# Last down projection: 14 of 22 k tiles of three pairs of output tiles as a block product by seven products

## The reference

```python
def conv_glu_ffn(xn, w_up, conv_w, conv_b, w_down):
    u = causal_dwconv3(xn @ w_up, conv_w) + conv_b
    gate, up = jnp.split(u, 2, axis=-1)
    return (jax.nn.silu(gate) * up) @ w_down
...
        x = x + conv_glu_ffn(rmsnorm(x, ffn_norm[layer]), ffn_w_up[layer], ffn_conv_w[layer],
                             ffn_conv_b[layer], ffn_w_down[layer])
```

## Time and profile before

| | us |
|---|---|
| median of 3 runs | 1110.01 |
| span of the profiled execution | 1108.5 |
| TensorE busy | 1103.2 |
| VectorE busy | 602.4 |
| ScalarE busy | 499.7 |
| GpSimd busy | 461.9 |

### The profile page before, as it was taken

One profiled execution on the slowest core, in us unless ns is written; L12 is line 12 of the kernel. 1 busy time (PEld: TensorE's weight loads), 2 busy tenths in 40 slices (PEclk: granted clock), 3 DMA queues, 4 the chain that ended last, 5 costly groups with the idle time before them and its releaser, 6 DMA issues.

```text
span 1108.5 us, 15680 instructions
## 1 busy us (share of the span) xinstructions
PE 1103.2 (100%) x5230; PEld 941.6 (85%) x5230; DVE 602.4 (54%) x1083; ACT 499.7 (45%) x808; POOL 461.9 (42%) x221
## 2 busy tenths in 40 slices
PE   9999999999999999999999999999999999999998
PEld 7888888888888888889999999888888888888887
DVE  6787775545454542125788888878645454540000
ACT  6233444444444432234777778644544444442120
POOL 4345534443534355443233233144544435344442
PEclk9999999999999999999999999999999999999999
DMA  7233322323222243333222333132323222224331
GB/s 267 77 114 97 114 76 97 111 91 98 95 95 87 62 112 98 94 98 114 76 77 82 101 94 96 48 108 82 133 78 111 90 99 95 78 67 116 91 106 74
DMA packets 47704, 108.16 MB, mean 98 GB/s; under 512 B 4752, under 2 KB 20368, under 8 KB 47664
## 3 DMA queue, kind: packets, MB, share of 16 engines
q1 hardware_dynamic: 45184, 103.37, 29.6%
q10 hardware_dynamic: 2480, 4.27, 1.4%
HBM read 105.48 MB, written 2.15 MB: 97 GB/s over the span
## 4 chain that ended last, share of the span: by engine, by line
PE 97%; DVE 2%; ACT 0%; DMA 0%; issue 0%; SPq 0%; DVEq 0%; ACTq 0%
PE bank L1255 17%; PE bank L1256 17%; PE bank L1257 17%; PE spt L1255 8%; PE spt L1257 8%; PE spt L1256 8%; PE bank L1441 4%; PE bank L1443 4%; PE bank L1442 4%; PE obank L1544 2%; PE spt L1526 1%; PE spt L1515 1%; PE spt L1516 1%; PE obank L1257 1%; PE obank L1255 1%; PE obank L1256 1%
## 5 line engine op out<-in xcount | busy, mean ns | idle before, releaser
L475 POOL TENSOR_TENSOR wl<-raw,wh 128x1024 fp32r<-128x1024 f32 (+2 forms) x214 | 457.6, 2144 | 622.7 <-ACT wh L510 622.5
L1256 PE MATMUL bank<-xl,wh 128*128 128x512 f32 x776 | 301.9, 389 | 0.0
L1255 PE MATMUL bank<-xh,wh 128*128 128x512 f32 x776 | 301.9, 389 | 0.0
L1257 PE MATMUL bank<-xh,wl 128*128 128x512 f32 x776 | 301.9, 389 | 0.0
L510 ACT ACTIVATE wh<-raw 128x1024 fp32r<-128x1024 f32 (+2 forms) x214 | 201.9, 946 | 159.2 <-PE spt L1257 138.7
L1028 DVE TENSOR_TENSOR work<-bank,rstd 128x512 f32<-128x512 f32 x88 | 60.6, 691 | 217.7 <-PE bank L1257 217.7
L1255 PEld LDWEIGHTS bank<-xh,wh 128*128 128x128 f32 x776 | 145.7, 188 | 30.5
L1257 PEld LDWEIGHTS bank<-xh,wl 128*128 128x128 f32 x776 | 145.7, 188 | 30.3
L1256 PEld LDWEIGHTS bank<-xl,wh 128*128 128x128 f32 x776 | 145.7, 188 | 30.0
L1255 PE MATMUL spt<-bh,wh 128*128 128x512 f32 x408 | 158.8, 389 | 0.0
L1257 PE MATMUL spt<-bh,wl 128*128 128x512 f32 x408 | 158.7, 389 | 0.0
(11 more groups left out here) (181 smaller groups left out, 1257.2 us busy)
## 6 DMA issues: line engine op xcount, KB each, us to landing
raw<-w_up SPq DMA_DIRECT2D x88, 512.0 KB, 3.3
raw<-w_down SPq DMA_DIRECT2D x32, 384.0 KB, 3.1
raw<-w_qkv SPq DMA_DIRECT2D x32, 384.0 KB, 3.4
raw<-w_down SPq DMA_DIRECT2D x32, 320.0 KB, 2.9
raw<-w_in SPq DMA_DIRECT2D x14, 512.0 KB, 3.4
raw<-w_out SPq DMA_DIRECT2D x8, 512.0 KB, 3.2
work<-bias_rows ACTq DMA_DIRECT2D x16, 256.0 KB, 3.9
raw<-w_o SPq DMA_DIRECT2D x8, 512.0 KB, 4.1
```

The source lines that it names most:

```text
L475: nc.gpsimd.tensor_tensor(wl[s][:, 0:n], raw[s][:, 0:n], plain(wh[s][:, 0:n]), ALU.subtract).then_inc(s_lo, 1)
L1255: mm(dst, wh[s][:, w], hi, start=first, stop=False)
L1256: mm(dst, wh[s][:, w], lo, start=False, stop=False)
L1257: return mm(dst, wl[s][:, w], hi, start=False, stop=last)
```

## The change

Tiles 0 and 1 stay as they are, but now ScalarE rounds their later units in between other work. The other six tiles are three pairs. In each pair the weights of the first 14 k tiles are four pieces of 7 k tiles: a and b (upper tile, k 0 to 6 and 7 to 13), c and d (lower tile). The hidden activation is four pieces too: h11, h12 (k 0 to 6, left and right 256 tokens), h21, h22 (k 7 to 13). Instead of eight products of pieces there are seven, in the order a h11, b h21, (a+c+d) N2, (a+c) T3, (c+d) N1, (a+b+c+d) h22, d T4, with T3 = h22 - h12, N1 = h11 - h12, N2 = -T3 - h11, T4 = -N2 - h21. A product is 7 k tiles by two matmuls: wh against the high and the low part of the right-hand side side by side (2 x 256 columns, a bank), and wl against the high part (256 columns). VectorE folds the two halves of the banks into x. The last 8 k tiles of each tile stay plain ("upper", "lower").

The right-hand sides T3, N1, N2 and T4 are formed once, in four groups of k tiles (0 and 1, 2 and 3, 4 and 5, 6) by VectorE, rounded by ScalarE and their rests taken by VectorE; some of the values lie in PSUM banks meanwhile. They reuse xh, xl and the room of the former work tile (t_rest). The sums of weights are made by VectorE in the raw slots. ScalarE copies the running sum of the chain bank out three times a pair. SyncE's stores now stand between loads. xh, xl and the units' ring stay; bh and bl, and acc and sq, become halves of one tensor each, at no other size.

```diff
@@ sizes
+HALVED = 7
+FORMS = ("a", "b", "acd", "ac", "cd", "upper", "abcd", "d", "lower")
+FORM = {name: n for n, name in enumerate(FORMS)}
+UNITS = U_FORM + (PAIRED := KT // 2 - 1) * len(FORMS)
+SIDE = SEQ // 2
...
+T_GROUPS = ((0, 1), (2, 3), (4, 5), (6,))
...
@@ banks and pieces
+        cd_sum = acc_sq[:, 0:HALVED * P]
+        kept_up, kept_left = rstd, bv_sb[:, 0:SEQ]
+        chain_bank, right_bank, lower_bank = bank[0], bank[1], bank[2]
+        plain_bank = rbank
+        t_bank = (bank[3][:], nbank, obank[:])
...
@@ sync
+            for s, name in enumerate("abcd"):
+                sp.wait_ge(s_lo, U_DOWN1 + RING + s + 1)
+                piece_load(1, name)
+            for pair in range(1, PAIRED + 1):
+                rest_made(pair, "acd")
+                sp.wait_ge(s_v, sum_ready(pair, "abcd"))
+                piece_load(pair, "lower")
+                rest_made(pair, "ac")
+                piece_load(pair, "upper")
+                store(2 * pair - 2)
+                store(2 * pair - 1)
+                if pair < PAIRED:
+                    for name, before in (("a", "upper"), ("b", "abcd"), ("c", "d"), ("d", "lower")):
+                        rest_made(pair, before)
+                        piece_load(pair + 1, name)
+            store(KT - 2)
...
@@ gpsimd
+            rests(U_DOWN1, U_FORM, DOWN)
+            for pair in range(1, PAIRED + 1):
+                for name in FORMS:
+                    u, src = form_unit(pair, name), form_source(pair, name)
+                    n = src.shape[1]
+                    pool.wait_ge(s_hi, u + 1)
+                    nc.gpsimd.tensor_tensor(wl[u % RING][:, 0:n], src, plain(wh[u % RING][:, 0:n]),
+                                            ALU.subtract).then_inc(s_lo, 1)
...
@@ scalar
+            def round_t(g):
+                group = T_GROUPS[g]
+                for form, made, src in ((T3, 1, t_values(group)[2]), (N1, 3, t_sums(t_bank[1], group)),
+                                        (N2, 4, t_sums(t_bank[2], group)), (T4, 4, t_sums(t_bank[0], group))):
+                    act.wait_ge(s_traw, 4 * g + made)
+                    nc.scalar.activation(t_part(group, form, 0).bitcast(F32R), src, ACT.Copy).then_inc(s_thi, 1)
+            def keep_sum(pair, name, dst):
+                act.wait_ge(s_unit, form_unit(pair, name) + 1)
+                nc.scalar.activation(dst, chain_bank[:], ACT.Copy).then_inc(s_kept_sum, 1)
+            def last_down():
+                ahead(U_DOWN1, 0, 1, DOWN)
+                round_t(0)
+                ahead(U_DOWN1, 0, 2, DOWN)
+                ahead(U_DOWN1, 0, 3, DOWN)
+                round_t(1)
+                ahead(U_DOWN1, 1, 0, DOWN)
+                round_form(1, "a")
+                round_t(2)
+                round_form(1, "b")
+                round_t(3)
+                round_form(1, "acd")
+                for pair in range(1, PAIRED + 1):
+                    round_form(pair, "ac")
+                    if pair > 1:
+                        act.wait_ge(s_x, 3 * KT + 2 * pair - 1)
+                    else:
+                        act.wait_ge(s_tlo, 4 * len(T_GROUPS))
+                    keep_sum(pair, "a", kept_up[:])
+                    round_form(pair, "cd")
+                    if pair > 1:
+                        act.wait_ge(s_x, 3 * KT + 2 * pair)
+                    keep_sum(pair, "acd", kept_left)
+                    round_form(pair, "upper")
+                    round_form(pair, "abcd")
+                    round_form(pair, "d")
+                    act.wait_ge(s_upper, pair)
+                    keep_sum(pair, "cd", kept_up[:])
+                    round_form(pair, "lower")
+                    if pair < PAIRED:
+                        round_form(pair + 1, "a")
+                        round_form(pair + 1, "b")
+                        round_form(pair + 1, "acd")
...
@@ vector
+            def t_forms(g):
+                group = T_GROUPS[g]
+                def value(dst, lower, right):
+                    return nc.vector.tensor_tensor(dst, plain(h_part(group, lower, right, 0)),
+                                                   plain(h_part(group, lower, right, 1)), ALU.add)
+                h12, h21, t3 = t_values(group)
+                h22 = t4 = t_sums(t_bank[0], group)
+                h11 = n1 = t_sums(t_bank[1], group)
+                n2 = t_sums(t_bank[2], group)
+                link(value(h12, 0, 1))
+                link(value(h22, 1, 1))
+                nc.vector.tensor_tensor(t3, h22, h12, ALU.subtract).then_inc(s_traw, 1)
+                link(value(h11, 0, 0))
+                dve.wait_ge(s_traw, 4 * g + 1)
+                nc.vector.scalar_tensor_tensor(n2, t3, -1.0, h11, ALU.mult, ALU.subtract).then_inc(s_traw, 1)
+                nc.vector.tensor_tensor(n1, h11, h12, ALU.subtract).then_inc(s_traw, 1)
+                link(value(h21, 1, 0))
+                dve.wait_ge(s_traw, 4 * g + 3)
+                nc.vector.scalar_tensor_tensor(t4, n2, -1.0, h21, ALU.mult, ALU.subtract).then_inc(s_traw, 1)
+                for n, (form, src) in enumerate(((T3, t3), (N1, n1), (N2, n2), (T4, t4))):
+                    dve.wait_ge(s_thi, 4 * g + n + 1)
+                    nc.vector.tensor_tensor(t_part(group, form, 1).bitcast(F32R), src, t_part(group, form, 0),
+                                            ALU.subtract).then_inc(s_tlo, 1)
...
+            def weight_sum(pair, name):
+                def piece(which):
+                    return form_source(pair, {"a": "a", "b": "b", "c": "ac", "d": "d"}[which])
+                if name == "cd":
+                    for which in "cd":
+                        s, landed = raw_place[pair, which]
+                        dve.wait_ge(s_raw[s], landed)
+                    if pair > 1:
+                        dve.wait_ge(s_lo, form_unit(pair - 1, "cd") + 1)
+                    dst, one, two = cd_sum, piece("c"), piece("d")
+                elif name == "ac":
+                    s, landed = raw_place[pair, "a"]
+                    dve.wait_ge(s_raw[s], landed)
+                    dve.wait_ge(s_v, sum_ready(pair, "cd"))
+                    dst, one, two = piece("c"), piece("a"), piece("c")
+                elif name == "acd":
+                    dve.wait_ge(s_lo, form_unit(pair, "a") + 1)
+                    dve.wait_ge(s_v, sum_ready(pair, "ac"))
+                    dst, one, two = piece("a"), cd_sum, piece("a")
+                else:
+                    dve.wait_ge(s_lo, form_unit(pair, "b") + 1)
+                    dve.wait_ge(s_v, sum_ready(pair, "acd"))
+                    dst, one, two = piece("b"), piece("a"), piece("b")
+                nc.vector.tensor_tensor(dst, one, two, ALU.add).then_inc(s_v, 1)
...
+            def last_pair(pair):
+                upper, lower = 2 * pair, 2 * pair + 1
+                left, right = sides
+                done(pair, "b")
+                joined(pair, 1, kept_up[:], right_bank)
+                dve.wait_ge(s_joined, 3 * pair - 2)
+                fold(upper, left, halves(kept_up), ALU.add).then_inc(s_upper, 1)
+                done(pair, "cd")
+                joined(pair, 3, kept_up[:], lower_bank)
+                dve.wait_ge(s_joined, 3 * pair - 1)
+                link(fold(lower, right, halves(kept_up), ALU.subtract))
+                done(pair, "upper")
+                dve.wait_ge(s_upper, pair)
+                link(nc.vector.tensor_tensor(x[:, upper, :], plain_bank[0], x[:, upper, :], ALU.add))
+                done(pair, "abcd")
+                fold(upper, right, halves(chain_bank), ALU.add).then_inc(s_x, 1)
+                if pair < PAIRED:
+                    for name in ("cd", "ac", "acd"):
+                        weight_sum(pair + 1, name)
+                done(pair, "d")
+                joined(pair, 2, kept_left, lower_bank)
+                dve.wait_ge(s_joined, 3 * pair)
+                link(fold(lower, left, halves(kept_left), ALU.subtract))
+                if pair < PAIRED:
+                    weight_sum(pair + 1, "abcd")
+                done(pair, "lower")
+                if pair < PAIRED:
+                    nc.vector.tensor_tensor(x[:, lower, :], plain_bank[1], x[:, lower, :], ALU.add).then_inc(s_x, 1)
+                else:
                     for n, side in enumerate(sides):
-                        nc.vector.tensor_tensor(x[:, KT - 1, side], rbank[1][:, side], x[:, KT - 1, side],
+                        nc.vector.tensor_tensor(x[:, lower, side], plain_bank[1][:, side], x[:, lower, side],
                                                 ALU.add).then_inc(s_last[n], 1)
+            def last_down():
+                t_forms(0)
+                t_forms(1)
+                add_residual(0, U_DOWN1 + 4, rbank[0])
+                t_forms(2)
+                for name in ("cd", "ac", "acd"):
+                    weight_sum(1, name)
+                t_forms(3)
+                weight_sum(1, "abcd")
```

(85 more changed lines are left out.)

73 lines of the change are left out of this document (66 added, 7 removed).

## The result

The changed kernel takes 1130.49 us (median of 4 runs, 1129.7 to 1131.21) against 1110.09: a ratio of 1.0183, 95% interval 1.0169 to 1.0198, 20.4 us slower. The forecast was 1127.5, range 1120 to 1134. The span of the profiled execution is 1128.6.

A forecast was written before the change was run, and what follows sets the result against it. The prediction took TensorE, busy for the whole span, to bound the kernel. From 1110.0 us it added 22.7 of stalls, took off 6.2 of TensorE work and added 1.0 for the clock: 1127.5 us, range 1120 to 1134.

The forecast's parts named there:

- The step that decided: Before "acd" of pair 1, VectorE needs 32.7 us of bare work in 26.4, so is 6 us late without waits.
- the port's waits: VectorE's instructions reading two SBUF tiles wait out the GpSimd instruction they meet, as one took 2.09 us instead of 0.68.
- The four gaps: TensorE stalls 0.7 and 3.0 us at tile 1's units, 6.0 at "b" and 8.8 at "acd" of pair 1.
- The prediction's heading: It said the order on ScalarE, with weight roundings behind roundings of right-hand sides, moves each wait on.
- The clock: TensorE's clock falls to half at the two long gaps before "b" and "acd", costing 1.0 us, bounds 0 and 2.8.
- The load of "upper": In each pair it waits for GpSimd's "ac" and lands 3.3 us later, making "upper" late, 4.2 us together.
- TensorE's own work: With 256-column matmuls 0.12 us apart, a product takes 2.43 us, a pair 27.9 instead of 29.92; three pairs save 6.2.
- rival 2: In the products, 256-column matmuls are bound by their weight load, 0.19 us busy, giving 1133 us; chance 5%.
- Rival 1: VectorE and GpSimd do not block each other while forming right-hand sides; stalls 9.4 us in all, giving 1113; chance 5%.
- rival 3: Right-hand sides and "acd" are ready before 1020.36, TensorE never waits, the saving is whole: 1103.8 us; chance 3%.
- rival 4: Only the setting-up stalls; "upper" loads in time in the pairs, about 1124.7 us; inside the forecast's own range, no separate chance.
- The sum: Over the last down projection: stalls 22.7 us less 6.2 saved, +16.5, plus 1.0 for the clock, giving 1127.5 us.

The follow-up runs named there:

- experiment 1: Changed kernel without forming, rounding or awaiting the right-hand sides, their four products run on hidden-activation pieces instead: 1109.95 us, ratio 1.0001 to the kernel before.
- experiment 2: Changed kernel with each group's four sums bh + bl reading bh and a PSUM bank instead of two SBUF inputs: 1123.77 us, ratio 1.0126 to the kernel before.
- experiment 3: Changed kernel with ScalarE rounding tile 1's later units and forms "a" and "b" before the right-hand sides they stood behind: 1130.46 us, ratio 1.0181 to the kernel before.
- experiments 6 and 7: 6 is e_warm, 1129.66 us; 7 is the changed kernel with "upper" loaded first and idle matmuls only before "b" and "acd", 1122.52 us.
- e_warm: Changed kernel with idle TensorE matmuls before "b" and "acd" of pair 1 and before "upper" in each pair: 1129.66 us, ratio 1.0181 to the kernel before.
- experiment 4: Changed kernel with "upper" loaded into the slot that is free first and "lower" into the other: 1124.63 us, ratio 1.0132 to the kernel before.
- experiment 8: Changed kernel with block products for the last two pairs only, tiles 0 to 3 plain, "upper" loaded first: 1107.68 us, ratio 0.9979 to the kernel before.

## Why the prediction was right

- **The step that decided held.** It was VectorE's bare 32.7 us up to the end of the last group against 26.4 us of TensorE, with the port's waits on top. Measured were 31.6 of bare work and 8.0 of waits: VectorE was through with its last rest at 1033.5 (forecast 1035.6), and "acd" came at 1036.6 (forecast 1038.9). Experiments 1 and 2 split the loss into the forming as such and the port's share of 6.7 us.
- **The four gaps** were forecast at 0.7, 3.0, 6.0 and 8.8 us, 18.5 together; they were 0, 2.2, 5.1 and 6.3, 13.6. The first was missing, since ScalarE had rounded the second unit at 1002, in time. The four are one lateness seen four times: they add up to 1038.9 less 1020.4, when "acd" was ready and when it was due without any gap. The prediction's heading puts them down to ScalarE's order; experiment 3 shows that the order only decides where the lateness shows, since without the earlier gaps the last is 15.1 of wait.
- **The clock** was mis-sized. Forecast 1.0 (bounds 0 and 2.8); half speed took 5.9 us, 2.2 of it at "b", which counts for nothing, as forecast. It shows in the gaps, though: of the 4.9 us between 18.5 and 13.6, the slow "b" fills 2.2, and "acd" being ready 2.3 earlier than forecast, VectorE 2.1, is most of the rest. "acd" lost 2.0 and got it back at "upper", by experiments 6 and 7 as the prediction argued; the fall in pair 2, 1.7, was not foreseen.
- **The load of "upper".** Forecast 2.1, 1.1 and 1.1 (4.2 in its sum, 4.3 as they stand); measured 1.2, 2.4 and 1.9. The term used 3.3 us to landing, the median of loads of w_up, no two of which are issued within 2.3 us. Here the median of "lower" and "upper" was 4.3, and "upper" alone took 4.7 in pair 1 and 5.3 in pairs 2 and 3:

```profile
raw<-w_down SPq DMA_DIRECT2D x8, 448.0 KB, 3.4
raw<-w_down SPq DMA_DIRECT2D x6, 512.0 KB, 4.3
```

  In pairs 2 and 3 "lower" and "upper" are issued 0.4 us apart, since the sum "abcd", 2.9 us long beside GpSimd, comes last; the prediction had "upper" wait for GpSimd's "ac" there too. Pair 1's was less than forecast, since the half-speed "acd" filled part of it: in e_warm, at full clock, "upper" starts at 1047.16 and the product ahead of it ends at 1044.41, 2.8 us apart.
- **TensorE's own work.** A 256-column matmul behind a 512-column one is 0.12 as read off, and rival 2 is out (starts 1040.95 and 1041.07 below). But the 512-column matmul behind the narrow one takes 0.23 to 0.24 instead of 0.2266: a product is 2.46 instead of 2.43 and a pair without gaps 28.1 to 28.3 instead of 27.9. The saving is 1.6 to 1.8 us a pair, not 2.06. TensorE's timeline of the changed kernel, at half clock and at full:

```profile
1039.96 0.63 PE L1736 MATMUL bank<-t_rest,wh 128*128 128x512 f32 x1
1040.39 0.41 PE L1738 MATMUL bank<-t_rest,wl 128*128 128x256 f32 x1
1040.60 0.51 PE L1736 MATMUL bank<-t_rest,wh 128*128 128x512 f32 x1
1040.95 0.28 PE L1738 MATMUL bank<-t_rest,wl 128*128 128x256 f32 x1
1041.07 0.39 PE L1736 MATMUL bank<-xh,wh 128*128 128x512 f32 x1
1041.30 0.28 PE L1738 MATMUL bank<-xh,wl 128*128 128x256 f32 x1
```

- **The other rivals.** Rival 1 is out by the sums of 2 us and more, and rival 3 by the gaps. The condition of rival 4, a load of "upper" that lands in time, is nearly that of experiment 4, and its 1124.7 is what that measured (1124.6), in part by chance, since "upper" still waited 1.4 there and the half clock at "acd" cost 2.0 and not 2.4.
- **The sum.** Gaps 19.1 for a forecast 22.7, half clock 5.9 for 1.0, saving 5.0 (5.5 less the 0.5 behind the gaps) for 6.2: 20.0 for 17.5 in the profiled execution. Part of this only moved from gaps to half clock, as the forecast's 1.0 is what is left of the clock after it fills gaps. Counted by what was on the path, "acd" started 16.3 late for a forecast 18.5, and half clock and load in pair 1 cost 3.1, as forecast. Pairs 2 and 3 lost 6.0 at "upper" (4.3 of gaps, 1.7 of half clock) for a forecast 2.1, and the saving fell short by some 0.8. Errors of 2.2 one way and 4.7 the other: that the total was within 3 us is in part luck, that it lay far above the kernel before is not.

## What to carry to other kernels

An engine that is 90% idle over a stretch can still miss a deadline in it: add up the strictly ordered work between the moment its inputs exist and the moment the first consumer is due, here 40 us in 26. Where the deadline moves behind other work (experiment 8) the same instructions cost TensorE no wait, so ask first how early the new form is needed and on how many tiles it pays. And several waits in a row on one chain are one lateness, to be read at the last; the earlier ones are places at which it shows.

## What was not expected of the hardware

The granted clock fell in "upper" of pair 2 (0.50 from 1078.5 to 1081.5) behind a gap of only 2.4 us, and at the same place in experiment 3 (from 1078.0, also behind 2.4). It did not behind gaps of 2.2 at 1012, 1.9 at 1107, two of 2.2 in experiment 1 or two of 2.3 in experiment 2. The traces do not show what tells them apart, and it isn't the kernel alone: of ten runs of experiment 1 eight had a mean granted clock of 1.0, and the two with 0.998 took 1110.85 and 1111.18 us, 0.9 and 1.2 above the median. In the second long gap the clock stood at 1.00 from 1031 to 1034, when no matmul ran, and was at 0.50 again when "acd" began. So here the level read in an idle stretch was not the one that the next matmul got.

The Trainium skill ("TensorE: Matmul & The Clock Gate", "What's actually happening") says that the engine's activity sets the clock, over windows that run freely beside the kernel. These gaps fit that, in that like lengths had unlike results; no run here shows the cause.
